# Prompt attention of a decoder layer: unscaled probabilities in two float16 halves as the stationary operand

## The reference, cut to what matters

```python
o_cmp = einsum('bghtn,bngd->btghd', pc, vc)          # over 16 compressed blocks
p2 = softmax(where(m2, s2, NEG_INF))                  # "slc": here all earlier keys
o_slc = einsum('bghtnl,bgtnld->btghd', p2, g[..., 1, :])
...
p = softmax(where(m, s, NEG_INF))                     # "win": the last 512 keys
o_win = einsum('bnghtk,bnkgd->bntghd', p, vb)
o_att = (nsa_g[:, :, 0, :, :, None] * o_cmp + nsa_g[:, :, 1, :, :, None] * o_slc
         + nsa_g[:, :, 2, :, :, None] * o_win)
attn_out = o_att.reshape(B, T, Q_COLS) @ w_attn_up
```

## Time and profile before

| | |
|---|---|
| time, median of 3 runs | 2806.14 us (2804.74 to 2807.46) |
| span of the profiled execution | 2805.9 us |
| TensorE matmul busy | 2634.8 us, 94% |
| VectorE, ScalarE, GpSimd busy | 898.5, 648.9, 1261.5 us |
| attention over the prompt | 1120 to 1426 us of the span |

### The profile page before, as it was taken

One profiled execution on the slowest core, in us unless ns is written; L12 is line 12 of the kernel. 1 busy time (PEld: TensorE's weight loads), 2 busy tenths in 40 slices (PEclk: granted clock), 3 DMA queues, 4 the chain that ended last, 5 costly groups with the idle time before them and its releaser, 6 DMA issues.

```text
span 2805.9 us, 49857 instructions
## 1 busy us (share of the span) xinstructions
PE 2634.8 (94%) x19658; PEld 1805.4 (64%) x19658; DVE 898.5 (32%) x1364; ACT 648.9 (23%) x1388; POOL 1261.5 (45%) x949
## 2 busy tenths in 40 slices
PE   7999999999968999999986999999969999999997
PEld 3666666666648944677754666666646666666665
DVE  2323222210074343445421541222272232232104
ACT  3311111100043233665420101111251111110002
POOL 2378778843432331333323884343334443443431
PEclk9999999999989955999997999999989999999998
DMA  6133333321101431000033332111102111111111
GB/s 235 32 98 95 97 97 97 98 73 41 51 8 39 152 103 44 1 1 2 1 113 99 105 97 56 49 52 53 42 16 61 51 46 52 52 53 52 51 31 61
DMA packets 298364, 179.46 MB, mean 64 GB/s; under 512 B 8847, under 2 KB 288773, under 8 KB 298176
## 3 DMA queue, kind: packets, MB, share of 16 engines
q1 hardware_dynamic: 282780, 156.15, 19.0%
q0 software_dynamic: 3840, 11.54, 1.3%
q10 hardware_dynamic: 11620, 10.04, 1.1%
HBM read 170.81 MB, written 11.10 MB: 65 GB/s over the span
## 4 chain that ended last, share of the span: by engine, by line
PE 86%; DVE 6%; ACT 4%; issue 2%; DMA 1%; SPq 0%; POOL 0%; POOLq 0%; ACTq 0%; DVEq 0%
PE banks L224 23%; PE banks L225 23%; PE banks L226 23%; PE banks L1828 4%; PE banks L1464 2%; PE banks L1697 2%; PE banks L1803 2%; ACT pair L521 1%; DVE rs L577 1%; PE banks L320 1%; ACT ahi L524 1%; PE banks L1826 1%; DVE y L594 1%; PE banks L2116 1%; DVE pair L617 1%
## 5 line engine op out<-in xcount | busy, mean ns | idle before, releaser
L224 PE MATMUL banks<-ahi,whi 128*128 128x344 f16 x2784 | 866.4, 311 | 25.1 <-ACT sg L876 14.4
L225 PE MATMUL banks<-alo,whi 128*128 128x344 f16 x2784 | 866.2, 311 | 0.0
L226 PE MATMUL banks<-ahi,wlo 128*128 128x344 f16 x2784 | 865.9, 311 | 0.0
L215 POOL TENSOR_SCALAR stage<-stage 128x1024 f32<-128x1024 f32 (+1 forms) x248 | 273.6, 1103 | 979.2 <-PE banks L226 909.6
L220 POOL TENSOR_TENSOR wlo<-stage,whi 128x1024 f16<-128x1024 f32 (+1 forms) x248 | 543.9, 2193 | 20.7
L224 PEld LDWEIGHTS banks<-ahi,whi 128*128 128x128 f16 x2784 | 273.9, 98 | 163.1 <-issue 16.2
L226 PEld LDWEIGHTS banks<-ahi,wlo 128*128 128x128 f16 x2784 | 274.1, 98 | 136.8
L225 PEld LDWEIGHTS banks<-alo,whi 128*128 128x128 f16 x2784 | 273.9, 98 | 133.6 <-issue 0.6
L224 PE MATMUL banks<-hhi,whi 128*128 128x344 f16 x1056 | 326.3, 309 | 3.2 <-DVE hlo L937 3.2
L226 PE MATMUL banks<-hhi,wlo 128*128 128x344 f16 x1056 | 326.3, 309 | 0.0
L225 PE MATMUL banks<-hlo,whi 128*128 128x344 f16 x1056 | 326.3, 309 | 0.0
(11 more groups left out here) (308 smaller groups left out, 3539.6 us busy)
## 6 DMA issues: line engine op xcount, KB each, us to landing
stage<-in_w_ffn_gu_dram SPq DMA_DIRECT2D x88, 512.0 KB, 3.8
stage<-in_w_ada_dram SPq DMA_DIRECT2D x56, 512.0 KB, 3.8
stage<-in_w_ffn_down_dram SPq DMA_DIRECT2D x32, 704.0 KB, 4.6
stage<-in_w_in_dram SPq DMA_DIRECT2D x38, 512.0 KB, 3.8
first<-in_w_ada_dram SPq DMA_DIRECT2D x4, 2048.0 KB, 12.9
xrow<-in_x_prompt_dram ACTq DMA_DIRECT2D x8, 512.0 KB, 7.7
stage<-in_phi_w_dram SPq DMA_DIRECT2D x8, 512.0 KB, 4.2
ring<-in_state_win_kv_dram SPq DMA_DIRECT2D x16, 256.0 KB, 3.4
```

Of the source, the lines that this page charges most:

```text
L215: pool.tensor_scalar(st, st, WS, 1.0, ALU.mult, ALU.mult).then_inc(slab_scaled, 1)
L224: pe.matmul(out, w_hi, a_hi, start=start, stop=False)
L225: pe.matmul(out, w_hi, a_lo, start=False, stop=False)
L226: return pe.matmul(out, w_lo, a_hi, start=False, stop=stop)
```

## The change

The operands of the value product change places and type. The exponents are not scaled before they are turned. The turned ones are multiplied by 16384 and split into a float16 high half (ScalarE) and low half (VectorE); 128x128 of these stand in TensorE, and 64 columns of the values, split into halves behind their projection, move past them: three products per block. So the outputs come out as rows (128 queries by 64 columns of a head, bank 7). There, once for two heads, VectorE multiplies by inverse sum, gate and 1/16384, and GpSimd adds the branches to the row. The compressed branch is one product of 512 columns a tile, put into the row by ScalarE. A finished tile of rows is turned by four transposes and split. Probabilities have one buffer per kind instead of two. Transposes come one step sooner (TL 2 instead of 3), their evacuation too (EV 3 instead of 4), value products as well (PL 4 instead of 5). All transposes and the compressed product share a ring of three banks (4 to 6), taken in turn by `turn_bank`; bank 6 and bank 7 had other uses before. GpSimd's multiplication and its semaphore go, and the waits that named them.

```diff
-        vst = place("vst", [P, 2, TT + 1, P], F32)
+        vhl = place("vhl", [P, 2, 2, TT, P], F16)
+        vnew = place("vnew", [NDEC, 2, P], F32)
...
+            if n in (7, 9):
+                br = (n - 7) // 2
+
+                @block.scalar
+                def _(act):
+                    act.wait_ge(S("z_row"), evac[n])
+                    act.activation(vhl[:, br, 0], vrow[:, br, 0:TT, :], ACT.Copy).then_inc(S("v_hi"), 1)
+
+                @block.vector
+                def _(dve):
+                    dve.wait_ge(S("v_hi"), br + 1)
+                    dve.tensor_tensor(vhl[:, br, 1], vrow[:, br, 0:TT, :], vhl[:, br, 0], ALU.subtract)\
+                       .then_inc(S("v_lo"), 1)
+                    dve.tensor_copy(vnew[:, br, :], vrow[0:NDEC, br, TT, :]).then_inc(S("v_lo"), 1)
...
+        TL, EV, PL = 2, 3, 4
...
+        def turn_bank(pe):
+
+            i = len(ring_lo)
+            if i >= 3:
+                pe.wait_ge(S("t_hi"), i - 2)
+                if ring_lo[i - 3]:
+                    pe.wait_ge(S("t_lo"), ring_lo[i - 3])
+            return bank[4 + i % 3]
+
+        def turn_group(split):
+            i = len(ring_lo)
+            ring_lo.append(count("t_lo") if split else 0)
+            return i
...
+            @block.scalar
+            def _(act):
+                act.wait_ge(S("s_max"), at("s_max"))
+                earlier = [w for w in turned if units[w][0] == kind]
+                if earlier:
+                    act.wait_ge(S("t_mm"), turned[max(earlier)])
+                if t >= 2:
+                    act.wait_ge(S("o_scaled"), (t - 1) * NH // 2)
+                act.activation(probs_of(u), scores(u), ACT.Exp, bias=stat[:, u % 4:u % 4 + 1],
+                               accum_out=sums[:, t % 2, KINDROW[kind], h:h + 1]).then_inc(S("p_exp"), 1)
+            s_free[u] = prob_ready[u] = ("p_exp", count("p_exp"))
...
+        def turn(v):
+            kind, t, h = units[v]
+            n = 1 if kind == "cmp" else len(blocks(kind, t))
+            unit_groups[v] = []
+            for c in range(0, n, 4):
+                m = min(4, n - c)
+                    b = turn_bank(pe)
+                    pe.wait_ge(S(prob_ready[v][0]), prob_ready[v][1])
+                    for i in range(m):
+                        last = pe.transpose(b[:, i * P:(i + 1) * P], probs_of(v)[:, (c + i) * P:(c + i + 1) * P],
+                                            const("ident"))
+                    last.then_inc(S("t_mm"), 1)
+                unit_groups[v].append(turn_group(kind != "cmp"))
+            turned[v] = len(ring_lo)
...
+        def turned_hi(v):
...
+                earlier = [w for w in pv_done if w % 2 == v % 2]
+                if earlier:
+                    act.wait_ge(S("pv"), pv_done[max(earlier)])
+                n = len(blocks(kind, t))
+                for c, i in zip(range(0, n, 4), unit_groups[v]):
+                    m = min(4, n - c)
+                    act.wait_ge(S("t_mm"), i + 1)
+                    act.activation(pth[:, v % 2, c:c + m, :].rearrange("p m q -> p (m q)"), bank[4 + i % 3][:, 0:m * P],
+                                   ACT.Copy, scale=PS).then_inc(S("t_hi"), 1)
+
+        def turned_lo(v):
+            kind, t, h = units[v]
+            if kind == "cmp":
+                return
+
+            @block.vector
+            def _(dve):
+                n = len(blocks(kind, t))
+                for c, i in zip(range(0, n, 4), unit_groups[v]):
+                    m = min(4, n - c)
+                    dve.wait_ge(S("t_hi"), i + 1)
+                    dve.scalar_tensor_tensor(out=ptl[:, v % 2, c:c + m, :].rearrange("p m q -> p (m q)"),
+                                             in0=bank[4 + i % 3][:, 0:m * P], scalar=PS,
+                                             in1=pth[:, v % 2, c:c + m, :].rearrange("p m q -> p (m q)"),
+                                             op0=ALU.mult, op1=ALU.subtract).then_inc(S("t_lo"), 1)
+
+        def weighted(v):
+            kind, t, h = units[v]
+            if kind == "cmp":
+                @block.tensor
+                def _(pe):
+                    b = turn_bank(pe)
+                    pe.wait_ge(S("t_hi"), unit_groups[v][0] + 1)
+                    pe.matmul(b, pct[:, t % 2, :], vbd[:].rearrange("p h d -> p (h d)"), start=True, stop=True)\
+                      .then_inc(S("t_mm"), 1)
+                ocmp_group[t] = turn_group(False)
+                return
+            g, br, pair = h // HPG, KINDROW[kind], t * NH // 2 + h // 2
+            o = bank[7][:, br * 128 + h % 2 * 64:br * 128 + h % 2 * 64 + 64]
+
+            @block.tensor
+            def _(pe):
+                pe.wait_ge(S("t_lo"), ring_lo[unit_groups[v][-1]])
+                if kind == "slc" and h % 2 == 0 and pair >= 1:
+                    pe.wait_ge(S("o_scaled"), pair)
+                ks = blocks(kind, t)
+                for i, k in enumerate(ks):
+                    cols_ = slice(g * HD, (g + 1) * HD)
+                    pe.matmul(o, pth[:, v % 2, i, :], vhl[:, br, 0, k, cols_], start=i == 0, stop=False)
+                    pe.matmul(o, pth[:, v % 2, i, :], vhl[:, br, 1, k, cols_], start=False, stop=False)
+                    last = pe.matmul(o, ptl[:, v % 2, i, :], vhl[:, br, 0, k, cols_], start=False, stop=i == len(ks) - 1)
+                last.then_inc(S("pv"), 1)
+            pv_done[v] = count("pv")
+
+        def pair_shares(v):
+            kind, t, h = units[v]
+            pair, hs = t * NH // 2 + h // 2, slice(h - 1, h + 1)
+
+            @block.vector
+            def _(dve):
+                gates = gs[:, t, NH:3 * NH].rearrange("p (b h) -> p b h", b=2)[:, :, hs]
+                dve.wait_ge(S("p_exp"), prob_ready[v][1])
+                dve.reciprocal(shares[:, pair % 2], sums[:, t % 2, :, hs]).then_inc(S("share"), 1)
+                dve.wait_ge(S("share"), 2 * pair + 1)
+                dve.tensor_tensor(shares[:, pair % 2], shares[:, pair % 2], gates, ALU.mult).then_inc(S("share"), 1)
+                dve.wait_ge(S("share"), 2 * pair + 2)
+                dve.wait_ge(S("pv"), pv_done[v])
+                if pair >= 2:
+                    dve.wait_ge(S("o_add"), 2 * (pair - 1))
+                dve.scalar_tensor_tensor(
+                    out=opart[:, pair % 2].rearrange("p b h d -> p (b h) d"),
+                    in0=bank[7][:, 0:256].rearrange("p (b d) -> p b d", d=HD), scalar=1.0 / PS,
+                    in1=shares[:, pair % 2].rearrange("p b h -> p (b h)").unsqueeze(2).to_broadcast([P, 4, HD]),
+                    op0=ALU.mult, op1=ALU.mult).then_inc(S("o_scaled"), 1)
+
+            @block.gpsimd
+            def _(pool):
+                row = orow[:, t % 2, (h - 1) * HD:(h + 1) * HD]
+                two = opart[:, pair % 2].rearrange("p b h d -> p b (h d)")
+                pool.wait_ge(S("o_scaled"), pair + 1)
+                pool.tensor_tensor(two[:, 0], two[:, 0], two[:, 1], ALU.add).then_inc(S("o_add"), 1)
+                pool.wait_ge(S("o_add"), 2 * pair + 1)
+                pool.wait_ge(S("t_hi"), ocmp_group[t] + 1)
+                pool.tensor_tensor(row, row, two[:, 0], ALU.add).then_inc(S("o_add"), 1)
+
...
+        def rows_turn(t):
+            @block.tensor
+            def _(pe):
+                b = turn_bank(pe)
+                pe.wait_ge(S("o_add"), (t + 1) * NH)
+                for c in range(KC):
+                    last = pe.transpose(b[:, c * P:(c + 1) * P], orow[:, t % 2, c * P:(c + 1) * P], const("ident"))
+                last.then_inc(S("t_mm"), 1)
+            orow_group[t] = turn_group(True)
+
...
+        RL = 4
...
+            if unit(0) is not None:
+                score_unit(u)
+            if unit(TL) is not None:
+                turn(u - TL)
+            if unit(PL) is not None:
+                weighted(u - PL)
+            if row_end(PL + RL) is not None:
+                rows_turn(row_end(PL + RL))
+            if unit(PL + 1) is not None and units[u - PL - 1][0] == "win" and units[u - PL - 1][2] % 2 == 1:
+                pair_shares(u - PL - 1)
+            if unit(0) is not None:
+                greatest(u)
+            if unit(EV) is not None:
+                turned_hi(u - EV)
+            if unit(PL + 1) is not None and units[u - PL - 1][0] == "cmp":
+                compressed_row(units[u - PL - 1][1])
+            if row_end(PL + RL + 1) is not None:
+                rows_hi(row_end(PL + RL + 1))
+            if unit(0) is not None:
+                exponent(u)
+            if unit(1) is not None and units[u - 1][0] == "cmp":
+                compressed_shares(u - 1)
+            if unit(EV) is not None:
+                turned_lo(u - EV)
+            if row_end(PL + RL + 1) is not None:
+                rows_lo(row_end(PL + RL + 1))
```

More of the change, by code:

```diff
@@ L1588, in mixer, with scores, probs_of @@
         U = len(units)
-        probs, slot_before = [], []
-        for u, (kind, t, h) in enumerate(units):
-            turn = t if kind == "cmp" else h
```

(59 more changed lines are left out.)

315 lines of the change are left out of this document (132 added, 183 removed).

## The result

The changed kernel takes 2830.69 us (median of 4 runs, 2830.15 to 2835.5) against 2806.8 us for the one before (4 runs on the same chip): ratio 1.0088, 95% interval 1.0074 to 1.0103. It is slower, as predicted (2835, range 2812 to 2872). The profiled executions have spans of 2828.5 and 2805.9 us.

A forecast was written before the change was run, and what follows sets the result against it. The prediction took TensorE to bound the kernel (86% of the span). Its terms, 25.7 for tiles 4 to 7, -7 for tiles 0 to 3, +8 clock, +2 rest, made +29 on 2805.9: 2835 us, range 2812 to 2872.

The forecast's parts named there:

- The ring's wait: Tiles 4 to 7: TensorE's second transposes wait for VectorE's reduction and low half, 2.15 us (1024 columns) or 1.74 (640).
- Price of a product: Value products on TensorE: 29 ns each, 0.088 us a block, bounds 0.078 and 0.168.
- Rival 1: Tiles 4 to 7: second group finds its bank free, low half early enough; 147 us there, 2740 us total; chance 0.07.
- Tiles 0 to 3: First four tiles: VectorE bounds, 95.5 us against 102.7, so -7 us (bounds -27 and +1).
- The drain: End of attention: the last unit's operations one after the other, about 9.5 us after the last scores.
- The clock: Tiles 4 to 7: granted clock falls behind each of four compressed units, 2 us each, +8 (bounds 0 and +93).
- steps: Tiles 4 to 7: heads of 5.90, 6.35, 6.80 and 7.27 us, eight each, 210.6 us; compressed units add net 12.
- Terms of tiles 4 to 7: Last four tiles: +25.7 us for steps and drain (228.8 against 203.1), and +8 for the clock.
- Start and rest: Values' split at the projections' end +1 us, GpSimd's later page loads behind attention +1, each 0 to 2.

The follow-up runs named there:

- experiment 2: Changed kernel with VectorE's low half of u-3 before the maximum of u, and ScalarE's high half of u-2 instead of u-3 ahead of the exponent: 2772.39 us.
- experiment 4: Kernel before the change, with only VectorE's copy that frees bank 7 moved behind the row maximum: 2870.65 us, ratio 1.0229.
- experiment 5: Changed kernel with the value products of u-4 ahead of the transposes of u-2 on TensorE: 2818.13 us.
- experiment 6: Changed kernel with the value products ahead of the transposes in tiles 4 to 7 only: 2806.64 us, ratio 0.9996.
- experiment 1: Changed kernel with one move, VectorE's low half of u-3 ahead of the row maximum of u: 2863.8 us, ratio 1.0206.
- the best order: Changed kernel with low half before maximum, high half of u-2, new rows' copy on ScalarE, products of u-3 not u-4 behind transposes: 2748.02 us.
- experiment 8: Changed kernel with only the copy of the new values' rows moved from VectorE to ScalarE: 2830.71 us.
- experiment 3: Changed kernel with only the first of the three value products, the other two left out: 2815.82 us.
- experiment 9: Kernel with low half before maximum, high half of u-2 and products first everywhere, plus the new values' rows copied on ScalarE: 2760.84 us against 2765.68.

## Why the prediction was right

*The ring's wait.* Shown by experiments 2 and 4, and in the trace to 0.1 us: long step of tile 7 3.94 us (predicted 4.03), short step 3.22 (3.24). Per tile, with the compressed unit: 47.8, 54.9, 56.9 for tiles 4, 5, 6 against 50.2, 53.8, 57.4 predicted. Experiments 5 and 6 show the rest of the sentence in part: products that stand ahead of the wait instead of behind it gave 21 and 20 us in tiles 4 to 7, where 32 would have gone if all of them had become free.

*Price of a product.* Predicted 29 ns from half a 128-column slot; measured 29 ns at full clock and 53 ns at the low one (1393.12 to 1394.19). Weight load and product stream at that price with a 128x128 stationary each time. The Trainium skill ("TensorE: Matmul & The Clock Gate", Back-to-back issue gap) has such streams at about 81 ns for 128 moving columns. The trace has 56 ns for those, and 29 for 64. The 81 ns had no part in the sum.

*Rival 1.* The one mechanism that I said would decide, the low half ahead of the maximum, is not enough (experiment 1). I had looked at the order on one engine and not at what the low half itself waits for. Its price was not far off in the end: 147 us for tiles 4 to 7, where the best order reaches 153.2; the total of 2740 compares with 2748. That order is another one than the rival's, so the agreement is of VectorE's sum and not of the mechanism.

*Tiles 0 to 3*: -16.3 instead of -7, the largest miss. Tiles 2 and 3 were right (22.8 and 26.9 us against 23.3 and 27.5). Tiles 0 and 1 took 15.6 and 21.0 against 19 and 25.5: I had TensorE bound at the low clock for all of tile 0 and some of tile 1, but the clock rose during tile 0 (it was low again from 1141.7 to 1148.5, in tile 1; in experiment 8, with the same instructions and no such dip, tile 1 took 19.0 us instead of 21.0):

```profile
1123.80:1131.40 7.60, 5.45 (x43) 3.54 (x43) 3.97 (x16) 3.14 (x14) 0.00 (x0) 0.50 0.02 4
1131.40:1139.40 8.00, 6.14 (x78) 4.20 (x76) 6.75 (x28) 6.48 (x33) 1.82 (x4) 1.00 0.00 0
```

*The drain*: 13.75 us from the last scores, 9.5 predicted. I had followed the last unit alone; two units are still in the ring. The last long unit's second group waits its turn (1436.09), the products of the long unit before it stand behind that group (from 1436.55), and the last long unit's high halves wait for them because they use the same buffer. The same happens once more to the last short unit:

```profile
1437.45 1.09 ACT L1789 ACTIVATE pth<-banks 128x512 f16<-128x512 f32 x2 [2.02 <-PE banks L1832]
...
1439.65 0.77 ACT L1789 ACTIVATE pth<-banks 128x512 f16<-128x512 f32 x2 [1.11 <-PE banks L1832]
```

*The clock*: +8 for four dips behind the compressed units. There were three in tiles 4 to 7 (1264.6 to 1268.0, 1377.2 to 1380.6, 1387.4 to 1394.3), two of them in tile 7. The one in tile 5 begins 6.7 us and the last one 17.7 us into its tile, and tiles 4 and 6 have none, so that they stand behind the compressed units is not borne out. The excess of tiles 5 and 7 over their steps, 1.1 and some 4 us, is what I put down to them; the 1.4 us of one dip in tile 6 (experiment 3) fit that, but tile 7's 4 is what is left over, not measured. Terms of tiles 4 to 7 together: 25.7 + 8 predicted, 32.3 measured: drain 4.3 more, clock and steps each 2.9 less. That these parts cancel is luck.

*Start and rest*: +3.8 and +2.9 instead of +1 and +1. Of the start, the split costs 4.6 and an earlier arrival at this place gives 0.8 back (experiments 8 and 9). I had priced the split of the values by its columns and not the company it keeps: at the projections' end GpSimd splits the weights, and VectorE's 8x128 copy took 2.15 us, the four copies behind it 3.78 instead of 1.55. The copy ended at 979.40, GpSimd's 2.98 us instruction at 979.32. The Trainium skill, "SBUF — State Buffer", section SBUF: two separate sides, says that VectorE and GpSimd share a pair of ports as an exclusive lock, taken on VectorE's side by instructions in a 2-port mode or with two SBUF inputs, and that the loser blocks for the other's whole instruction. The two ends agree with it, and so does GpSimd's 2.98 us, which started beside VectorE's subtraction and took 2.15 in the kernel before; no run takes GpSimd's work away, so the lock itself is not shown here. The rest behind attention varies between 1380.1 and 1385.9 us over the kernels here, so of its +2.9 nothing can be assigned.

The net, +22.6 against +29, is then: tiles 0 to 3 9 us better than predicted, start and rest 5 worse, tiles 4 to 7 1 better (drain 4 worse, clock 3 better, steps 3 better, rounded).

## What to carry to other kernels

When a change adds a reader to a rotating buffer, write down for each engine what stands ahead of the release, and follow that back through the other engines until the chain reaches work that is already done; if it comes back to the newest scores, two engines alternate and the saved work turns into waiting. A wait in an in-order queue makes all behind it late and nothing ahead of it, so the cheap cures are orders, not fewer instructions: here nearly all of 83 us lay in the order of three kinds of steps, and 15 in two thirds of the products. Repair the whole cycle at once: the first move alone (experiment 1) made it 33 us worse.

## What the hardware showed that I had not expected

- A 128x128 weight load and a 64-column float16 product share a slot of 29 ns (a stream of 15 products from 1426.48); at the low clock (0.50, 1.2 GHz) it is 53 ns (20 slots of a stream of 24).
- Beside GpSimd's tensor-tensor instruction an 8x128 copy on VectorE takes 2.15 us; the same copy on ScalarE took 0.29.
- Less work on TensorE went with a lower granted clock in a stage that waits: 1.00 to 0.89 in tile 4 with one product of three, 0.92 to 0.88 in tiles 0 to 3, and below the changed kernel's over the span in each of six runs. With the best order it is 1.00 through tiles 4 to 7.
- Dips of the clock differ between executions of the same instructions, and their price can be read there: tile 1 took 21.0 us with a dip from 1141.7 to 1148.5 and 19.0 without, tile 6 58.4 with a dip and 57.0 without.
- A transfer issued 3.1 us earlier, 0.4 us behind a 512 KB load instead of 3.5, landed 0.7 us earlier.
